# Weights as half units of 512 KB in eight half buffers, norm gains by products, and loads and slots moved

## The chip, the core and the metric

The kernel runs on one core of one Trainium2 chip. The metric is the time of one execution on the device, in microseconds. It is float32 throughout.

## What is computed

A first block and a second block of a transformer run over one sequence of S = 256 tokens with D = 2048 features. The first block has one layer, the second two. Cut to what matters here:

```python
# first block, one layer
h = rms_norm(x, mix_norm_g)                      # gain per feature
proj = h @ w_in                                  # latents, q, k, v of 16 "fox" heads, gates
y_a = causal_block_attention(q_a, k_a, v_a)      # 16 heads from latents, with rope
y_b = causal_block_attention(q_b, k_b, v_b, cum_log_f)
x = x + (concat(y_a, y_b) * sigmoid(gates + b_gate)) @ w_out
h2 = rms_norm(x, ffn_norm_g)
x = x + peer_ffn(h2, ...)                        # see below

# second block, two layers
proj = x @ w_in
ya = diff_attention(...); yb = dilated_attention(...)
yc = conformer_conv(u, glu_gate, ...)            # 31 taps, layer norm over 512 channels, swish
y = concat(ya * silu(ag), yb * silu(bg), yc * silu(cg)) @ w_out
x = layer_norm(ALPHA * x + y, ln_g, ln_b)
```

`peer_ffn` picks, for each token, 8 heads times 16 experts out of 16,384: queries by `w_peer_q`, scores against two sets of 128 keys, the 16 best pairs. Each chosen expert is a row of 2048 numbers of `peer_u` (a dot product with h2, then gelu and the gate's weight) and a row of `peer_v` (added to x with that weight). So each token reads 128 rows of either table.

## The kernel before

**Tiles and passes.** The tokens are two tiles t = 0, 1 of 128. The program is eight passes in this order: `layer1(0)`, `experts(0)`, `layer1(1)`, `experts(1)`, `layer2(0, 0)`, `layer2(1, 0)` (both layers of the second block for tile 0), `layer2(0, 1)`, `layer2(1, 1)`. Each pass streams all its weights from memory. All five engines have an instruction stream written out by hand; semaphores tie them.

**The weight stream.** A unit is a tile of 128 partitions by 2048 floats (8 KB a partition, 1 MB), in the order of `order1` and `order2` (L85 to L111). `STREAM` lists all 612 units with what frees each. SP loads unit u into `ring[:, u % 4]` once PE has used unit u - 4 (L991). On PE `units` (L1339), `out_units` (L1373) and `fin_units` (L1381) wait for a unit and run four matmuls of 512 columns on it: `units` sums a chunk of 512 columns into `psP` over four units, the other two add the merged heads times `w_out` into the four banks of `psO`. ACT or DVE take the chunks. L1339 is hence the line of most matmuls.

**The rows of the experts.** 1024 indirect loads would be one per token and expert; here one gather brings one row for each of the 128 tokens of a tile, 1 MB, so there are 512 gathers: 128 of `peer_u` and 128 of `peer_v` for each tile. POOL issues them in order (L944), each into one of six buffers `rows` or a seventh in `hrow`, once DVE has used the row that was there. DVE uses a row in `slot`: L363 for the dot product, L371 for the addition to `x_sb`. The slots of tile 0 stand among the steps of `layer1(1)` and the start of `experts(1)`, those of tile 1 from there to the end of `layer2(1, 0)`. `stage(m)` opens a stretch of m slots and `mix(f)` runs slots up to the fraction f of it, so a call of `mix` is a point in DVE's order. The counts are tables: `MIX1`, `EMIX`, `MIX2`. In `layer2(l, 0)` each slot is followed by one tap of the convolution (L387) until 31 are done; for tile 1 POOL computes the convolution (L957 to L963).

**The experts' start (tile 1).** `experts(t)` on DVE (from L680) takes transposes, waits for `rsx_ready` (the root of the mean square, by ACT), and forms `hrow` = h2. For t = 0 this is x times the root times a row of gains that was loaded. For t = 1 PE transposes `hT`, which holds x times the gain, back in `rows_back` (L1658) within the second chunk, and DVE multiplies what stands in `psX` by the root (L698). Then come `mix(1.0)` (10 slots) and four rounds of finding the best 16, each of which gives POOL 32 more gathers.

**The convolution's norm.** The mean over 512 channels is a product of `ones` with each of four 128-channel blocks of `cacc` summed in `psX` (L1713), then the same for the squares `csq` (L1718).

**Start and norm rows.** SP loads x of tile 0; ACT loads the identity (L1049) and the 16 columns of `mix_g` (L1050); POOL loads the rest of the constants once x is in. In `layer2(0, 1)` ACT issues, ahead of its first chunk, the bias and counts for the far keys (L1225, L1226) and the four rows `ln_g`, `ln_b` of both layers (L1228).

## Time and profile before

| | us |
|---|---|
| median of 3 runs | 3230.13 |
| lowest, highest | 3229.79, 3232.44 |
| the profiled execution: time | 3231.43 |
| its span, first to last instruction | 3229.6 |
| PE busy | 2475.9 (77%) |
| DVE busy | 1874.4 (58%) |
| POOL busy | 928.7 (29%) |
| ACT busy | 459.2 (14%) |
| bytes moved | 1193.46 MB, 370 GB/s over the span |

The profile is of one execution. Its page gives busy time of the engines and what moved in 40 equal slices of the span; views of the trace give the same for any stretch, list who waited for whom, and print instructions in order of time.
### The profile page before, as it was taken

What the parts mean: (1) busy time and instruction counts of PE and PEld (TensorE: products, weight loads), DVE (VectorE), ACT (ScalarE), POOL (GpSimd) and SP (SyncE); (2) the same over time, 40 slices, a digit from 0 to 9 for tenths busy, and PEclk for the clock granted to TensorE, in tenths of its full rate; (3) what the DMA queues carried; (4) which work ended last, traced back from release to release, by engine and by line L of the source; (5) the groups of instructions that cost most, each with busy time, mean ns of one, the idle gap of its engine ahead of it and who ended that gap; (6) DMA issues with size and microseconds to landing.
All of it is one profiled execution on the core that took longest, in us unless ns stands there. A gap on an engine that the chain in (4) does not pass through costs nothing.

```text
span 3229.6 us, 19340 instructions
## 1 busy us (share of the span) xinstructions
PE 2475.9 (77%) x6564; PEld 1172.0 (36%) x6564; DVE 1874.4 (58%) x2830; ACT 459.2 (14%) x1126; POOL 928.7 (29%) x649
## 2 busy tenths in 40 slices
PE   8999999837757767576788276555645689999998
PEld 4444444413323333233333123222322234444443
DVE  1332333967576576665698857674985653452533
ACT  3222122111101110111101001010100111111111
POOL 0000000345343344333333334431432323500710
PEclk9999999967878888887999698788878889999999
DMA  9888887999999999999999999999999998887886
GB/s 333 279 293 274 286 284 275 418 421 418 421 416 420 422 417 421 422 421 417 356 416 421 404 422 421 422 413 421 421 400 422 421 376 331 290 293 274 279 285 232
DMA packets 169553, 1193.46 MB, mean 370 GB/s; under 512 B 18600, under 2 KB 22328, under 8 KB 25328
## 3 DMA queue, kind: packets, MB, share of 16 engines
q1 hardware_dynamic: 90320, 644.13, 52.6%
q0 software_dynamic: 74192, 538.86, 40.3%
q10 hardware_dynamic: 4944, 9.25, 0.8%
q8 instruction: 52, 0.85, 0.1%
q14 instruction: 45, 0.37, 0.0%
HBM read 1190.07 MB, written 2.10 MB: 369 GB/s over the span
## 4 chain that ended last, share of the span: by engine, by line
DMA 20%; PE 17%; DVE 10%; issue 2%; POOL 2%; ACT 0%; DVEq 0%; ACTq 0%
PE psP L1339 13%; DMA rows<-in_peer_v,tk 11%; DMA rows<-in_peer_u,tk 8%; DVE x_sb L371 3%; PE psO L1373 3%; DVE rows L363 2%; POOL rows L944 2%; DVE work L387 1%; PE psO L1381 1%; DMA hrow<-in_peer_u,tk 1%; DVE hrow L363 0%; DMA ring<-in_w 0%; PE psX L1470 0%; POOL hrow L944 0%; DVE kv L676 0%
## 5 line engine op out<-in xcount | busy, mean ns | idle before, releaser
L1339 PE MATMUL psP<-ring,hT 128*128 128x512 f32 x3584 | 1636.2, 611 | 109.4 <-DMA ring<-in_w 104.8
L1339 PEld LDWEIGHTS psP<-ring,hT 128*128 128x128 f32 x3584 | 685.9, 196 | 990.2 <-issue 812.5
L371 DVE SCALAR_TENSOR_TENSOR x_sb<-rows,tk,x_sb 128x2048 f32<-128x2048 f32 x223 | 524.4, 2351 | 237.8 <-DMA rows<-in_peer_v,tk 218.2
L944 POOL DMA_INDIRECT rows<-in_peer_u,tk x222 | 349.4, 1574 | 1074.6 <-DVEq L732 553.4
L363 DVE CUSTOM_DVE_ANT_0 rows<-rows,hrow 128x2048 f32<-128x2048 f32 x222 | 504.0, 2291 | 207.0 <-DMA rows<-in_peer_u,tk 202.4
L944 POOL DMA_INDIRECT rows<-in_peer_v,tk x223 | 332.5, 1491 | 576.6 <-DVE x_sb L371 511.1
L1373 PE MATMUL psO<-ring,work 128*128 128x512 f32 x832 | 384.2, 615 | 0.5 <-DMA ring<-in_w 0.5
L409 DVE STREAM_TRANSPOSE work<-work 32x128 f32<-32x128 f32 (+1 forms) x640 | 206.4, 323 | 147.4 <-ACT work L1235 87.7
L1373 PEld LDWEIGHTS psO<-ring,work 128*128 128x128 f32 x832 | 161.4, 199 | 187.4 <-issue 186.0
L1480 PE MATMUL psX<-kst,work 128*128 128x128 f32 x68 | 17.9, 415 | 253.0 <-DVEq L526 201.7
L1065 ACT ACTIVATE work<-work,small 128x256 f32<-128x256 f32 (+1 forms) x128 | 56.6, 444 | 481.0 <-DVEq L505 481.0
L1339 PE MATMUL psP<-ring,work 128*128 128x512 f32 (+1 forms) x288 | 114.5, 547 | 8.1 <-DMA ring<-in_w 8.1
L1480 PEld LDWEIGHTS psX<-kst,work 128*128 128x128 f32 x68 | 11.7, 207 | 266.4 <-DVEq L526 211.6
L371 DVE SCALAR_TENSOR_TENSOR x_sb<-hrow,tk,x_sb 128x2048 f32<-128x2048 f32 x33 | 77.6, 2351 | 35.7 <-DMA hrow<-in_peer_v,tk 32.3
L1447 PE MATMUL psX<-kv,work 128*128 128x128 f32 x128 | 28.9, 351 | 85.3 <-DVE kv L512 85.3
L363 DVE CUSTOM_DVE_ANT_0 hrow<-hrow 128x2048 f32<-128x2048 f32 x34 | 77.9, 2290 | 24.8 <-DMA hrow<-in_peer_u,tk 24.1
L1381 PE MATMUL psO<-ring,work 128*128 128x512 f32 x192 | 86.5, 608 | 1.9 <-ACT work L1078 1.4
L523 DVE SCALAR_TENSOR_TENSOR work<-psX,small,work 128x128 f32<-128x128 f32 x96 | 27.0, 345 | 98.3 <-PE psX L1470 97.8
L963 POOL TENSOR_TENSOR work<-work 128x512 f32<-128x512 f32 x60 | 76.3, 1272 | 4.7
L1339 PEld LDWEIGHTS psP<-ring,work 128*128 128x128 f32 x288 | 53.7, 190 | 65.0 <-issue 60.0
L944 POOL DMA_INDIRECT hrow<-in_peer_u,tk x34 | 49.9, 1467 | 86.0 <-DVE tk L363 64.5
L944 POOL DMA_INDIRECT hrow<-in_peer_v,tk x33 | 48.3, 1464 | 84.8 <-DVE x_sb L371 73.0
(352 smaller groups left out, 1622.6 us busy)
## 6 DMA issues: line engine op xcount, KB each, us to landing
ring<-in_w SPq DMA_DIRECT2D x572, 1024.0 KB, 9.0
ring<-in_wq SPq DMA_DIRECT2D x32, 1024.0 KB, 5.0
ring<-in_w SPq DMA_DIRECT2D x8, 512.0 KB, 5.4
rows<-in_peer_v,tk POOLq DMA_INDIRECT x223, 21.6
rows<-in_peer_u,tk POOLq DMA_INDIRECT x222, 20.1
x_sb<-in_x SPq DMA_DIRECT2D x2, 1024.0 KB, 5.9
rows<-in_gate_bias SPq DMA_DIRECT2D x1, 2048.0 KB, 12.2
work<-in_sub_keys ACTq DMA_DIRECT2D x2, 1024.0 KB, 7.9
```

Source lines behind the costliest of these rows:

```text
L363: V.tensor_tensor_reduce(out=row_buf(n), in0=row_buf(n), in1=hrow[:, t, :], scale=1.0, scalar=0.0, op0=ALU.mult, op1=ALU.add, accum_out=do ...
L371: V.scalar_tensor_tensor(out=x_sb[:, t, :], in0=row_buf(n), scalar=dots[t][:, k:k + 1], in1=x_sb[:, t, :], op0=ALU.mult, op1=ALU.add).then ...
L387: own.add(V.scalar_tensor_tensor(out=cacc[:, c, :], in0=convh[:, c, k:k + P], scalar=w, in1=cacc[:, c, :], op0=ALU.mult, op1=ALU.add))
L409: own.add(V.transpose(dst[b_:b_ + 32, :, a_:a_ + 32], src[a_:a_ + 32, :, b_:b_ + 32]))
L944: pool.indirect_dma_start(out=row_buf(n), out_offset=None, in_=a["peer_u" if s < SLOTS else "peer_v"], in_offset=bass.IndirectOffsetOnAxis ...
L963: own.link(T(cacc, cacc, csq, ALU.add))
L1065: ins = A(W4[:, j, :], W4[:, j, :], ACT.Exp, bias=negm[:, 4 * u + j:4 * u + j + 1], accum_out=lsum[:, 4 * u + j:4 * u + j + 1])
L1339: last = MM(psP[:, c % 2, 0:wide], src[:, kk, :], w[:, k, :], start=(kk == 0 and not begun), stop=(kk == 4 * nu - 1))
L1373: last = MM(psO[:, d, :], src[:, k, :], w[:, d, :], start=(bool(first) and k == 0), stop=False)
L1381: last = MM(psO[:, d, :], src[:, k, :], w[:, k, :], start=False, stop=(k == 3))
L1447: last = MM(o, qT[:, j, :], kT[:, j, :], start=(kind != "fox"), stop=(kind != "fox" or bank_ends))
L1480: last = TR(psX[:, 0, P * j:P * (j + 1)], mN[:, P * j:P * (j + 1)], ident)
```

## The change

1. **Half units.** `RING` is 8 buffers of 1024 floats a partition. Each unit becomes two loads and two waits on PE: two matmuls per half. `small` becomes twice 640 floats, `r` twice 512. x of tile 0 comes in two halves too.
2. **Start.** The 16 columns `mix_g` stand beside the identity and come with it in one load; POOL's constants wait for the first half unit, not for x.
3. **Experts of tile 1.** In place of the transposes back, PE forms the gain of every feature in all partitions, 16 matmuls of the broadcast gain columns with the identity into `psO`, between the first two units and the third of its first chunk; DVE multiplies x, root and gain in one operation. Four of the ten slots (`mix(0.4)`) go ahead of it.
4. **Convolution's norm for tile 1.** DVE adds the four blocks up first (two reductions), and PE then needs one matmul for the sum and one for the squares.
5. **Loads one by one.** Bias and counts follow chunk `u`; the four norm rows are issued singly, behind chunks q and v of groups 0 and 1.
6. **Slots moved.** `MIX2` has four fewer in group 1 and four more in group 2 of each layer.

```diff
-RING = 4
+RING = 8
+HALF = UNIT // 2
-MIX2 = [[20, 37, 59], [43, 36, 49]]
+MIX2 = [[20, 33, 63], [43, 32, 53]]
...
+        _h = width(_name) // 2
+        _ended["used"] += 1
+        STREAM.append((_p, _row, 0, _h, "used", _ended["used"]))
         _ended[_how] += 1
-        STREAM.append((_p, _row, width(_name), _how, _ended[_how]))
+        STREAM.append((_p, _row, _h, _h, _how, _ended[_how]))
...
-        ring = sb("ring", [P, RING, UNIT])
+        ring = sb("ring", [P, RING, HALF])
...
                 dve.wait_ge(rsx_ready, t + 1)
                 if t == 0:
                     dve.wait_ge(grow_in, 16)
+                else:
+                    mix(0.4)
                 for d in range(4):
                     w = slice(512 * d, 512 * (d + 1))
                     if t == 1:
-                        dve.wait_ge(h2T_done, d + 1)
-                        V.tensor_scalar(hrow[:, 1, w], psX[:, d % 2, :], rsh[:, 1:2], None, ALU.mult).then_inc(h2T_taken, 1)
-                        continue
-                    own.add(V.scalar_tensor_tensor(out=hrow[:, t, w], in0=x_sb[:, t, w], scalar=rsh[:, t:t + 1], in1=grow[:, w],
-                                                   op0=ALU.mult, op1=ALU.mult))
+                        dve.wait_ge(gain_done, d + 1)
+                    own.add(V.scalar_tensor_tensor(out=hrow[:, t, w], in0=x_sb[:, t, w], scalar=rsh[:, t:t + 1],
+                                                   in1=psO[:, d, :] if t else grow[:, w], op0=ALU.mult, op1=ALU.mult))
                 own.own()
                 if t == 1:
-                    dve.wait_ge(h2T_taken, 4)
+                    dve.sem_inc(gain_taken, 1)
                 mix(1.0)
...
                     if g == 2:
                         mix(0.24 * last)
+                        if t == 1:
+                            dve.wait_ge(conv_done, l + 1)
+                            link(V.tensor_reduce(crs, cacc.rearrange("p c s -> p s c"), AX, ALU.add))
+                            dve.sem_inc(csum_ready, 1)
                         dve.wait_ge(cm_done, r)
                         link(V.tensor_scalar(cmean, psX[:, 1, 0:P], 1.0 / 512, None, ALU.mult))
                         link(V.tensor_tensor(cacc, cacc, over(cmean, CC), ALU.subtract))
                         dve.sem_inc(cc_ready, 1)
                         if t == 1:
+                            dve.wait_ge(csq_ready, r)
+                            link(V.tensor_reduce(cmean, csq.rearrange("p c s -> p s c"), AX, ALU.add))
+                            dve.sem_inc(csum_ready, 1)
                             turn_k(kind, i, l, g)
...
-            pool.wait_ge(x_in, 16)
+            pool.wait_ge(arrived[0], 16)
...
-            sp.dma_start(x_sb[:, 0, :], a["x"][:, 0, :]).then_inc(x_in, 16)
-            for u, (p, row, n, how, count) in enumerate(STREAM):
+            sp.dma_start(x_sb[:, 0, 0:D // 2], a["x"][:, 0, 0:D // 2]).then_inc(x_left_in, 16)
+            sp.dma_start(x_sb[:, 0, D // 2:D], a["x"][:, 0, D // 2:D]).then_inc(x_in, 16)
+            for u, (p, row, at_, n, how, count) in enumerate(STREAM):
...
-                if u == 8:
+                if u == 16:
                     sp.dma_start(x_sb[:, 1, :], a["x"][:, 1, :]).then_inc(x1_in, 16)
...
-                act.dma_start(kst[:, 0:P], a["konst"][:, 0:P]).then_inc(first_in, 16)
-                act.dma_start(cols[:, 0:DC], a["cols"][:, 0:DC]).then_inc(first_in, 16)
+                act.dma_start(kst[:, 0:P + DC], a["konst"][:, 0:P + DC]).then_inc(first_in, 16)
...
-                    for dst, name, at_ in ((ln_g, "ln_g", D), (ln_b, "ln_b", D), (ln_g0, "ln_g", 0), (ln_b0, "ln_b", 0)):
-                        act.dma_start(dst, bass.AP(tensor=a[name].tensor, offset=at_, ap=[[0, P], [1, D]])).then_inc(lnrow_in, 16)
...
+                    if r == 3 and g < 2:
+                        ln_row((ln_g, ln_g0)[g], "ln_g", (D, 0)[g])
...
             def units(c, q0, q1, nu, src, wide=512, begun=False):
-                for q in range(q0, q1):
-                    w = v3(unit()[:, 0:4 * wide], wide)
-                    for k in range(4):
-                        kk = 4 * q + k
-                        last = MM(psP[:, c % 2, 0:wide], src[:, kk, :], w[:, k, :], start=(kk == 0 and not begun),
-                                  stop=(kk == 4 * nu - 1))
-                    last.then_inc(proj_ready if q == nu - 1 else unit_used, 1)
+                for kk in range(4 * q0, 4 * q1):
+                    if kk % 2 == 0:
+                        w = v3(unit()[:, 0:2 * wide], wide)
+                    last = MM(psP[:, c % 2, 0:wide], src[:, kk, :], w[:, kk % 2, :], start=(kk == 0 and not begun),
+                              stop=(kk == 4 * nu - 1))
+                    if kk % 2:
+                        last.then_inc(proj_ready if kk == 4 * nu - 1 else unit_used, 1)
...
+            def gain_over():
+
+                for d in range(4):
                     for j in range(4):
-                        last = TR(psX[:, r % 2, P * j:P * (j + 1)], hT[:, 4 * r + j, :], ident)
-                    last.then_inc(h2T_done, 1)
+                        last = MM(psO[:, d, P * j:P * (j + 1)], col("ffn_g", 4 * d + j).to_broadcast([P, P]), ident, start=True, stop=True)
+                    last.then_inc(gain_done, 1)
...
+                        if t:
+                            pe.wait_ge(csum_ready, 2 * l + 1)
+                            MM(psX[:, 1, 0:P], ones, crs, start=True, stop=True).then_inc(cm_done, 1)
```

The order on PE at the start of `experts(1)`, before; L1351 are the transposes of x, L1339 the query chunks, L1658 the transposes back, L1619 and L1628 the query transposes and the scores of a group:

```order
L1351 MATMUL psX<-kst,x_sb 128x128 x12
L1339 MATMUL psP<-ring,hT 128x512 x4
L1351 MATMUL psX<-kst,x_sb 128x128 x4
L1339 MATMUL psP<-ring,hT 128x512 x16
L1658 MATMUL psX<-kst,hT 128x128 x8
L1339 MATMUL psP<-ring,hT 128x512 x4
L1658 MATMUL psX<-kst,hT 128x128 x8
L1619 MATMUL psX<-kst,work 128x128 x4
L1339 MATMUL psP<-ring,hT 128x512 x4
L1628 MATMUL psO<-work 128x128 x4
```

and after the change:

```order
L1371 MATMUL psX<-kst,x_sb 128x128 x12
L1358 MATMUL psP<-ring,hT 128x512 x4
L1371 MATMUL psX<-kst,x_sb 128x128 x4
L1358 MATMUL psP<-ring,hT 128x512 x4
L1678 MATMUL psO<-kst,cols 128x128 x16
L1358 MATMUL psP<-ring,hT 128x512 x12
L1648 MATMUL psX<-kst,work 128x128 x4
L1358 MATMUL psP<-ring,hT 128x512 x4
L1659 MATMUL psO<-work 128x128 x4
```

The 16 products for the gain stand behind the second unit, and the transposes back are gone.

The order on ACT at the start of `layer2(0, 1)`, before; L1229 and L1230 take chunks `u` and `glu`, L1235 q, L1244 k, L1258 v:

```order
L1295 ACTIVATE small<-small 128x1
L1225 DMA kv<-in_bias_t 128x12x128
L1226 DMA rows<-in_log_count 128x2x128
L1228 DMA rows<-in_ln_g 128x2048
L1228 DMA rows<-in_ln_b 128x2048
L1228 DMA rows<-in_ln_g 128x2048
L1228 DMA rows<-in_ln_b 128x2048
L1229 ACTIVATE work<-psP 128x512
```

and after the change, where those lines are L1238, L1242, L1247, L1258 and L1272:

```order
L1315 ACTIVATE small<-small 128x1
L1238 ACTIVATE work<-psP 128x512
L1240 DMA kv<-in_bias_t 128x12x128
L1241 DMA rows<-in_log_count 128x2x128
L1242 ACT_TABLE_LOAD
L1242 ACTIVATE work<-psP 128x512
L1247 ACTIVATE work<-psP 128x512
L1303 DMA rows<-in_ln_g 128x2048
L1258 ACTIVATE work<-psP 128x512
L1271 ACTIVATE work<-psX 128x4x128
L1272 ACTIVATE work<-psP 128x512
L1303 DMA rows<-in_ln_b 128x2048
```

The first pair of norm rows stands behind q and v of group 0; the second pair stands the same way in group 1.

## Rows read from the trace of the kernel before

**Rows 1.** The page's second part, the span in 40 slices.

```profile
PE   8999999837757767576788276555645689999998
...
GB/s 333 279 293 274 286 284 275 418 421 418 421 416 420 422 417 421 422 421 417 356 416 421 404 422 421 422 413 421 421 400 422 421 376 331 290 293 274 279 285 232
```

**Rows 2.** Windows: stretch, length, busy us by engine, clock, DMA share, GB/s.

```profile
640.00:1520.00 880.00, 586.35 (x1517) 283.08 (x1517) 594.65 (x504) 115.20 (x316) 364.50 (x232) 0.80 1.01 420
1580.00:2640.00 1060.00, 643.79 (x1612) 293.29 (x1610) 784.06 (x1012) 92.40 (x198) 375.69 (x258) 0.84 1.01 418
2940.00:3200.00 260.00, 260.00 (x706) 123.09 (x705) 102.76 (x256) 35.07 (x74) 72.17 (x63) 1.00 0.82 283
```

**Rows 3.** The chain that ended last: start, us, what.

```profile
2730.85 27.66 PE psP L1339 x64
```

**Rows 4.** DMA queues from 563 to 2641 us: packets, MB, share.

```profile
q0 software_dynamic: 73728, 536.90, 62.4%
q1 hardware_dynamic: 44908, 324.55, 37.8%
```

**Rows 5.** PE's waits from 563 to 2641 us: total, times, longest.

```profile
PE psX L1480 <- DVEq L526: 201.7, 12, 28.5
PE psP L1339 <- DMA ring<-in_w: 107.2, 94, 2.7
```

**Rows 6.** The start: DMA issues to landing, and the timeline.

```profile
kst<-in_konst ACTq DMA_DIRECT2D x1, 64.0 KB, 5.4
cols<-in_cols ACTq DMA_DIRECT2D x1, 8.0 KB, 7.5
...
8.84 1.94 PE L1351 MATMUL psX<-kst,x_sb 128*128 128x128 f32 x8 [8.84 <-DMA cols<-in_cols]
```

**Rows 7.** PE's ring wait in the first stage, in the timeline.

```profile
46.93 13.97 PE L1339 MATMUL psP<-ring,hT 128*128 128x512 f32 x32 [1.92 <-DMA ring<-in_w]
```

**Rows 8.** Timeline of the experts of tile 1.

```profile
1542.10 0.20 ACT L1016 ACTIVATE small<-small 128x1 f32<-128x1 f32 x1
...
1557.98 0.66 PE L1619 MATMUL psX<-kst,work 128*128 128x128 f32 x4 [1.07 <-DVE hrow L698]
1558.02 19.54 DVE L371 SCALAR_TENSOR_TENSOR x_sb<-rows,tk,x_sb 128x2048 f32<-128x2048 f32 x8
...
1560.64 3.00 POOL L944 DMA_INDIRECT rows<-in_peer_v,tk  x1 [46.61 <-DVE x_sb L371]
```

**Rows 9.** Windows: 1550 to 1570 us.

```profile
1550.00:1570.00 20.00, 18.93 (x69) 9.94 (x67) 14.38 (x9) 1.28 (x2) 8.45 (x4) 1.00 0.76 271
```

**Rows 10.** Timeline of the convolution's norm, layer 0, tile 1.

```profile
2839.24 1.05 PE L1713 MATMUL psX<-work,kst 128*128 128x128 f32 x8
...
2840.14 7.03 PE L1339 MATMUL psP<-ring,hT 128*128 128x512 f32 x16
```

**Rows 11.** PE at the start of the last stage, the first of three waits.

```profile
2674.95 3.67 PE L1339 MATMUL psP<-ring,hT 128*128 128x512 f32 x8 [1.34 <-DMA ring<-in_w]
```

**Rows 12.** Layer 1 of tile 0: the keys of group 1, and the next window.

```profile
2397.74 2.05 PE L1447 MATMUL psX<-kv,work 128*128 128x128 f32 x8 [42.64 <-DVE kv L512]
...
2400.00:2420.00 20.00, 20.00 (x70) 10.91 (x70) 18.98 (x17) 1.65 (x8) 12.12 (x7) 0.99 0.89 336
```

**Rows 13.** Packets from 38.3 to 44.2 us, and from 44.5 to 50 us.

```profile
DMA packets 931, 2.40 MB, mean 408 GB/s; under 512 B 16, under 2 KB 16, under 8 KB 846
...
DMA packets 324, 2.33 MB, mean 425 GB/s; under 512 B 39, under 2 KB 39, under 8 KB 39
```

**Rows 14.** Packets from 1522 to 1536 us, with ACT's queue.

```profile
DMA packets 2364, 5.50 MB, mean 393 GB/s; under 512 B 110, under 2 KB 1798, under 8 KB 1798
...
q10 hardware_dynamic: 1746, 1.00, 24.3%
```

**Rows 15.** The queues from 1890 to 1920 us.

```profile
q1 hardware_dynamic: 870, 6.35, 51.0%
q0 software_dynamic: 863, 6.29, 50.3%
```

More of the change, by code:

```diff
@@ L48 @@
     NCOLS += _n
-KONST = [("ident", P), ("ones", P), ("tri", P), ("aid", P), ("mask", S), ("iota", TOPK), ("eps6", 1), ("eps5", 1),
+KONST = [("ident", P), ("mix_g", DC), ("ones", P), ("tri", P), ("aid", P), ("mask", S), ("iota", TOPK), ("eps6", 1), ("eps5", 1),
          ("lsc128", 1), ("lsc192", 1), ("one", 1)]
@@ L201, in col @@
         def col(name, i=0):
+            if name == "mix_g":
+                return kst[:, KOL[name] + i:KOL[name] + i + 1]
             return cols[:, COL[name] + i:COL[name] + i + 1]
@@ L1258, in layer2 @@
                     A(value_parts(kind, i, l, t)[-1], taken(("b", l, t, "v", g)), ACT.Copy).then_inc(chunk_taken, 1)
+                    if r == 3 and g < 2:
+                        ln_row((ln_b, ln_b0)[g], "ln_b", (D, 0)[g])
                     if t == 0:
@@ L1363, in x_first @@
                         turn(q + 2)
+                    elif q == 2 and between is not None:
+                        between()
                     units(c, q, q + 1, 4, hT)
@@ L1370, in out_units @@
                 for k in range(k0, k1):
-                    w = v3(unit(), 512)
                     for d in range(4):
-                        last = MM(psO[:, d, :], src[:, k, :], w[:, d, :], start=(bool(first) and k == 0), stop=False)
-                    last.then_inc(unit_used, 1)
+                        if d % 2 == 0:
+                            w = v3(unit(), 512)
+                        last = MM(psO[:, d, :], src[:, k, :], w[:, d % 2, :], start=(bool(first) and k == 0), stop=False)
+                        if d % 2:
+                            last.then_inc(unit_used, 1)
             def fin_units(src):
@@ L1378, in fin_units @@
                 for d in range(4):
-                    w = v3(unit(), 512)
                     for k in range(4):
-                        last = MM(psO[:, d, :], src[:, k, :], w[:, k, :], start=False, stop=(k == 3))
-                    last.then_inc(bank_done, 1)
+                        if k % 2 == 0:
+                            w = v3(unit(), 512)
+                        last = MM(psO[:, d, :], src[:, k, :], w[:, k % 2, :], start=False, stop=(k == 3))
+                        if k % 2:
+                            last.then_inc(bank_done if k == 3 else unit_used, 1)
             def no_a_step():
@@ L1518, in x_here @@
                     if r == 0:
[L1519 to L1520 removed]
+                        pe.wait_ge(first_in, 16)
+                    pe.wait_ge(x_left_in if r < 2 else x_in, 16)
                 if t == 0:
@@ L1527, in layer1 @@
                 c = begin(("a", t, "small", 0))
-                w = v3(unit()[:, 0:1280], 80)
                 for k in range(DC):
-                    last = MM(psP[:, c % 2, 0:80], hT[:, k, :], w[:, k, :], start=(k == 0), stop=(k == DC - 1))
+                    if k % 8 == 0:
+                        w = v3(unit()[:, 0:640], 80)
+                    last = MM(psP[:, c % 2, 0:80], hT[:, k, :], w[:, k % 8, :], start=(k == 0), stop=(k == DC - 1))
+                    if k == 7:
+                        last.then_inc(unit_used, 1)
                 last.then_inc(proj_ready, 1)
@@ L1710, in layer2 @@
                     if g == 2:
[L1711 to L1719 removed]
+                        if t:
+                            pe.wait_ge(csum_ready, 2 * l + 1)
+                            MM(psX[:, 1, 0:P], ones, crs, start=True, stop=True).then_inc(cm_done, 1)
+                        else:
+                            pe.wait_ge(conv_dve, l + 1)
+                            for m in range(CC):
+                                last = MM(psX[:, 1, 0:P], ones, cacc[:, m, :], start=(m == 0), stop=(m == CC - 1))
+                            last.then_inc(cm_done, 1)
+                        units(c, 0, 2, 4, hT)
+                        if t:
+                            pe.wait_ge(csum_ready, 2 * l + 2)
+                            MM(psX[:, 1, P:2 * P], ones, cmean, start=True, stop=True).then_inc(cv_done, 1)
+                        else:
+                            pe.wait_ge(csq_ready, r)
+                            for m in range(CC):
+                                last = MM(psX[:, 1, P:2 * P], ones, csq[:, m, :], start=(m == 0), stop=(m == CC - 1))
+                            last.then_inc(cv_done, 1)
                         units(c, 2, 4, 4, hT)
```

70 lines of the change are left out of this document (26 added, 44 removed).

## The prediction

> **What bounds the kernel now.** Read the page's second part first: its rows cut the span into 40 slices of some 81 us. Three stages show [rows 1]. In slices 1 to 7 and 34 to 40 PE is busy at nine tenths or more in nearly all, its clock nearly whole, and memory delivers 274 to 293 GB/s in most. In slices 8 to 33 PE is at two to eight tenths and memory at 413 to 422 in all but a few. The windows over these stages give the level: 283 GB/s with PE busy all the time, against 420 and 418 GB/s with PE busy 586 of 880 and 644 of 1060 us [rows 2]. So the ends are bound by PE (one unit of 1 MB shows as 8 matmul entries, 27.66 us for 64 of them in the chain, 3.46 us a unit [rows 3], 303 GB/s), and the middle by the DMA engines, which carry 536.9 MB of gathered rows beside 324.55 MB of weights [rows 4]. PE stands idle for some 710 us of the two middle windows, mostly for DVE, whose slots wait for rows (the largest group alone is 201.7 us); for the ring it waits 107.2 us in 94 short waits [rows 5]. What takes DMA time away in the middle, or fills a hole in it, therefore shifts the end one for one; at the ends only what holds PE counts. The profiled execution took 3231.4 us, its span 3229.6; the median of the runs is 3230.1, so 1.3 us come off the sum at the end.
>
> **The change, part by part.** *Start.* PE's first transpose waits for the small load of `mix_g`: it takes 7.5 us to land, the identity's, issued just ahead, 5.4, and PE begins at 8.84 [rows 6]. With `mix_g` in the identity's load, and x in halves, the last to land is that load, some 0.5 us of issue and 2.1 of landing sooner: **2.6 us less**, since PE is busy from there to the experts. Bounds: 0 (the wider load lands as late as the old pair) to 3. POOL's constant loads now wait for the first half unit and not for x, perhaps 1 us later; the first to need them is ACT's root for the first chunk, which PE finishes four units, 14 us [rows 3], after its first, so that is covered.
>
> *Ring at 45 us.* PE waits once for the ring in the first stage, 1.9 us, behind the 3 MB of x and gate bias on SP's queue [rows 7]. The first half of a unit is there 1.25 us before the whole (0.52 MB at 420 GB/s): **1.2 less**, 0 to 1.9.
>
> *Experts of tile 1.* DVE's root is ready when ACT ends at 1542.30, yet the rows are taken up at 1558.02, because DVE stands at the transposes back, and POOL had nothing to gather for 46.61 us [rows 8]. Now four slots stand ahead of that wait. The first can end at 1542.3 + 2.4 = 1544.7, where it ended at 1560.6: gathers restart 16 us sooner. A restart has a ramp, so I count only from 1550 to 1570: 271 GB/s against 421 for 20 us is 3.0 MB, or 7.1 us [rows 9]: **7 less**. Ends: 3 less (more ramp) and 16 less (DVE's own lead, which the DMA rate after 1580 forbids). PE swaps 16 transposes and 1.07 us of waiting [rows 8] for 16 true matmuls at 0.225 us (a group of 4 is followed 0.90 us later [rows 10]), 3.6 us, so at most 2.5 more, in a stretch where DVE and the DMA engines are behind: nothing. The scores of group 0 now wait for DVE to have read the gain from `psO`, which it does near 1555 (four slots of 2.44 us from 1542.3 and four short operations), ahead of PE's transposes for them, which stood at 1557.98 [rows 8].
>
> *Convolution norm of tile 1.* Four sums of 4 matmuls become 4 single ones: 12 times 0.225 us [rows 10], on PE in the last stage, **2.7 less**. DVE adds two reductions. The first waits for nothing but DVE's own order, since POOL's convolution is long done; should it be late, PE stands still. The second must be there when PE has run two units, 6.9 us after the first sums [rows 10]; between them lie a scaling, a subtraction, ACT's square and the reduction, each under 1 us. The key transpositions behind it on DVE start some 1.5 us later, and PE needs them two units and more after that. Hidden; were the cover gone, it would cost twice 1.5 us.
>
> *Norm rows of the second block.* Bias, counts and four rows of 1 MB go out together on ACT's queue, and PE then waits three times for the ring, 1.34, 1.55 and 0.93 us (the first of them: [rows 11]). Now bias and counts follow `u`, and the rows go out singly, a unit or more apart; the ring's cushion of 4 MB is over 13 us of PE. **3.8 less**, bounds 2 and 4.
>
> *Slots moved.* In the second block four slots go from group 1 to group 2 of each layer. PE waited 42.64 us there for the keys, which stood behind DVE's slots with their taps [rows 12]; it now waits behind three fewer (0.6 of 32 slots, not of 36). Only holes in the DMA stream count, and the following 20 us show one: 336 GB/s, 4.0 us [rows 12]. I take half, **2.0 less**, 0 to 4.
>
> *Halves.* Every unit is now two transfers of 4 KB a partition. No row shows such a stream, so it is bounded by its neighbours. While the gate bias loads, 931 packets (16 markers, 830 of 2 KB, so 85 of 8 KB) take 5.9 us; just behind it 324 (285 of 8 KB, 39 markers) take 5.5 us [rows 13]. Over 16 engines a packet of 8 KB costs 88 / 285 = 309 ns; the 830 cost (94.4 - 26.2) / 830 = 82 ns, where a quarter of 309 is 77. A line through both has a fixed part of 6.6 ns. Halving the packets adds one for each 8 KB: 324.55 MB [rows 4] are 39,600 of them, 2,480 per engine, at 6.6 ns **16.3 us more**. The farther neighbour is the bias load with rows of 512 bytes: 393 GB/s over 14 us [rows 14]. Its 5.50 MB less 1.00 leave 4.5 MB, 10.7 us at 421; the 1746 packets took 3.3 us, 30 ns each where the line through zero gives 19: a fixed part of 11 ns, 27 us. Lower end: 0, if the fixed part is hidden at 4 KB. A gain has no source in a stream that is already full. I take the 2 KB neighbour as the nearer one. At the ends memory has a fifth to spare, and nothing is lost. SP issues 1,224 loads in place of 612, at most one each 1.7 us of PE's work, and has nothing else to do. The Trainium skill ("DMA: Bandwidth & Descriptors", Bandwidth) speaks against the change: at least 1 MiB per DMA for three quarters of peak. This trace agrees only in part: four queued loads of 1 MiB reach 425 GB/s here [rows 13], far above the 341 stated there for one, so the size of a single transfer is not what limits. The same page of the Trainium skill (SWDGE vs HWDGE vs iDMA) gives 408.7 GB/s for a stream with rows of 4 KiB; an estimate by that page would be 324.55 MB at 408.7 in place of 425, some 30 us more and not 16.
>
> **Sum:** -2.6 - 1.2 - 7.0 - 2.7 - 3.8 - 2.0 + 16.3 = -3.0. From 3231.4 that is 3228.4, and 1.3 lower by the runs: **3227 us**. 0.2% is 6.5 us, about what a measurement of this kernel tells from no change: 3223.7 to 3236.6.
>
> **The rivals.** *A: packets of 4 KB cost nothing.* Then -19.3 stays: 3211. For it: the fixed part rests on 5.9 us of trace, and 1% of its rate is most of it. Against: both neighbours show one.
>
> *B: the packet costs as by the bias load,* 27 us: 3238.
>
> *C, slower: the share of the queues tips.* Where both queues are full, the two take turns packet by packet: 870 and 863 packets, 6.35 and 6.29 MB in 30 us [rows 15]. If weights bring 4 KB a turn and gathers 8, weights fall from 211 GB/s to 140, and a unit comes every 7.5 us, not 5.0. Each of the 94 ring waits grows by 2.5 us, 235 us in all. PE's other idle time, 600 us, covers most, and the DMA engines stay full while row buffers are free. It decides once DVE stands before PE with all seven full: then memory runs at PE's 303 of 421 GB/s and 28% is lost. With a quarter of the 235 us in that state it costs 16 us: 3243. The Trainium skill, "DMA: Bandwidth & Descriptors" (Queues, rings and completion order), has engines alternate between rows packet by packet; the trace agrees (870 against 863). It also has packets span several descriptors, by which the share need not follow the row's length.
>
> *D: the experts' hole stays,* since rows for the last slots land no sooner: 7 us back, 3234.
>
> **How the numbers follow.** Forecast 0.37 (own range 3219 to 3236), A 0.26, B 0.13, C 0.14, D 0.10. Faster: A whole and 0.11 of the forecast, 0.37. Slower: most of B and C and a little of D and the forecast, 0.27. Same: 0.36. The range leaves out a tenth at each side: 3208 to 3246.
>
> **What the profile after would show.** PE's first transpose near 6.2 us. POOL's longest gap in the experts of tile 1 near 30 us, not 46.6. No ring waits in the 50 us behind the last gather. In the middle the rate, now 418 to 420 GB/s over the long windows: 415 to 417 for the forecast, unchanged for A, 413 for B. For C: in stretches with both queues full twice as many bytes gathered as loaded, ring waits well over 107 us, and windows far under the stage's rate. Wrong outright, whatever the time, if the rate is the same and the gathers' restart is not.

## The result and the profile after

The change made the kernel slower: 3237.9 us median (3234.8 to 3242.3) against 3230.6 before (3227.3 to 3238.1), 17 runs each, a ratio of 1.0022 with a 95% interval of 1.0014 to 1.0029. Forecast were 3227 us and a range of 3208 to 3246: the time lies in the range, but the kernel is slower where a gain of 3 us was forecast. The profiled execution took 3242.3 us, the slowest of the 17; its span is 3240.2, where that of before was 3229.6. So the two traces differ by 10.6 us and the medians by 7.3.

The page of the kernel after, its second part, then the chain by line:

```profile
PE   9999999847666667566877555555665679999998
...
PEclk9999999978999999998999999999999999999999
...
GB/s 340 277 296 275 283 285 276 410 418 418 417 417 416 417 417 414 417 416 415 365 410 386 416 417 417 417 417 417 416 417 417 416 367 325 315 299 273 280 292 229
...
DMA ring<-in_w 38%; PE psP L1358 29%; PE psO L1396 7%; DMA rows<-in_peer_u,tk 7%; PE psO L1406 2%; DVE rows L369 2%; DMA ring<-in_wq 2%; DVE x_sb L377 1%; POOL rows L957 1%; PE psX L1473 1%; PE psX L1496 1%; PE psX L1371 1%; PE psX L1470 1%; PE psX L1469 0%; DMA rows<-in_peer_v,tk 0%
```

The three stages stand as before [rows 1], but no slice of the middle reaches 422 any more: the best are 418 and most 417. The chain (the work that ended last, followed back step by step) now runs over the ring for 38% of the span. PE's waits in the middle of the kernel after (line, what for: total, times, longest):

```profile
PE psP L1358 <- DMA ring<-in_w: 500.9, 305, 2.8
PE psO L1396 <- DMA ring<-in_w: 71.7, 46, 1.9
PE psX L1506 <- DVEq L532: 26.3, 2, 16.4
```

They answer to [rows 5]. PE waited 201.7 us for DVE at one place and 107.2 us for the ring; it now waits some 570 us for the ring and 26.3 for DVE in the largest such group. The queues from 1890 to 1920 us, after, against [rows 15]:

```profile
q0 software_dynamic: 1144, 8.32, 66.8%
q1 hardware_dynamic: 1141, 4.15, 34.7%
```

Still packet by packet, 1144 against 1141, and so two bytes gathered for each one loaded: the share that rival C named is there. The start, in PE's timeline:

```profile
5.04 1.97 PE L1371 MATMUL psX<-kst,x_sb 128*128 128x128 f32 x8 [5.04 <-DMA kst<-in_konst]
...
41.03 3.71 PE L1557 MATMUL psP<-ring,hT 128*128 128x80 f32 x16 [2.11 <-DMA ring<-in_w]
```

PE begins 3.8 us sooner than in [rows 6], yet waits 2.11 us at 41 us where it waited 1.92 at 47 [rows 7], and the first gather is issued at 562.1 us, 1.0 sooner.

**A ledger.** The stage between the first gather and PE's first transpose of tile 1's second block is bound by DMA and carries 864.0 MB (536.9 of rows, 324.4 of weights, 2.7 of the rest; after), and within 1 MB as much in the other kernels with the same gathers. Its length splits into the bytes at the full rate of that kernel's packets (422 GB/s with packets of 8 KB, 417 with weights in 4 KB, both shown below) and holes, the remainder: the time that would be over if memory had run at that rate throughout. The row of a kernel adds up to its span:

| kernel | first stage | bytes at full rate | holes | last stage | span |
|---|---|---|---|---|---|
| before | 563.1 | 2047.4 | 31.3 | 587.8 | 3229.6 |
| after | 562.1 | 2071.9 | 27.3 | 578.9 | 3240.2 |
| whole | 561.8 | 2047.4 | 26.2 | 580.8 | 3216.2 |
| halves | 565.2 | 2071.9 | 23.7 | 586.6 | 3247.4 |
| pieces | 564.9 | 2071.9 | 27.7 | 579.2 | 3243.7 |
| slots | 562.8 | 2047.4 | 22.9 | 579.5 | 3212.6 |
| oldexp | 560.4 | 2047.4 | 29.1 | 580.6 | 3217.5 |
| halves_exp | 561.0 | 2071.9 | 22.0 | 578.1 | 3233.0 |
| whole_exp | 561.0 | 2047.4 | 25.0 | 579.6 | 3213.0 |
| whole_late | 557.4 | 2047.4 | 27.3 | 580.7 | 3212.8 |
| best | 557.8 | 2047.4 | 23.5 | 579.0 | 3207.7 |

So after against before is -1.0 at the start, +24.5 by the rate, -4.0 in holes and -8.9 in the last stage. Each row is one execution, and kernels with the same start differ by up to 2.4 us in the first column, so differences under 3 us in a cell prove nothing. Between a kernel with packets of 8 KB and one with 4 KB the cut between rate and holes is no sharper: the streams alone moved 421.9 and 417.5 GB/s before rounding, and with these two the term for the rate is 22 us and not 24.5, and the holes of `after` are as many as before.

### The profile page after: what moved, and what is told of

It is laid out like the page before. It is cut to its first block, busy times and chain, and to the rows that moved or that the text cites. A ratio compares the mean times of both kernels' runs of the same rounds, so it can differ in the third digit from the quotient of the medians.

```text
span 3240.2 us, 19946 instructions
## 1 busy us (share of the span) xinstructions
PE 2488.9 (77%) x6556; PEld 1124.8 (35%) x6556; DVE 1881.8 (58%) x2834; ACT 458.5 (14%) x1126; POOL 908.9 (28%) x649
## 4 chain that ended last, share of the span: by engine, by line
DMA 47%; PE 44%; DVE 7%; issue 1%; POOL 1%; ACT 1%; DVEq 0%; ACTq 0%
DMA ring<-in_w 38%; PE psP L1358 29%; PE psO L1396 7%; DMA rows<-in_peer_u,tk 7%; PE psO L1406 2%; DVE rows L369 2%; DMA ring<-in_wq 2%; DVE x_sb L377 1%; POOL rows L957 1%; PE psX L1473 1%; PE psX L1496 1%; PE psX L1371 1%; PE psX L1470 1%; PE psX L1469 0%; DMA rows<-in_peer_v,tk 0%
## 5 line engine op out<-in xcount | busy, mean ns | idle before, releaser
L1358 PE MATMUL psP<-ring,hT 128*128 128x512 f32 x3584 | 1664.5, 610 | 481.0 <-DMA ring<-in_w 461.6
L1358 PEld LDWEIGHTS psP<-ring,hT 128*128 128x128 f32 x3584 | 659.7, 193 | 1414.8 <-issue 743.8
L957 POOL DMA_INDIRECT rows<-in_peer_u,tk x222 | 294.6, 1327 | 1128.0 <-DVEq L738 550.5
L957 POOL DMA_INDIRECT rows<-in_peer_v,tk x223 | 362.3, 1625 | 527.0 <-DVE x_sb L377 464.6
L1396 PEld LDWEIGHTS psO<-ring,work 128*128 128x128 f32 x832 | 153.0, 193 | 268.3 <-issue 173.2
L1358 PE MATMUL psP<-ring,work 128*128 128x512 f32 (+1 forms) x288 | 124.7, 575 | 39.3 <-DMA ring<-in_w 39.3
L957 POOL DMA_INDIRECT hrow<-in_peer_v,tk x33 | 58.0, 1757 | 82.2 <-DVE x_sb L377 76.4
L393 DVE SCALAR_TENSOR_TENSOR work<-work,cols 128x128 f32<-128x128 f32 x240 | 68.0, 346 | 0.0
L972 POOL TENSOR_TENSOR work<-work,cols 128x512 f32<-128x512 f32 x62 | 65.2, 1052 | 4.9
```

The source lines that it names most:

```text
L393: own.add(V.scalar_tensor_tensor(out=cacc[:, c, :], in0=convh[:, c, k:k + P], scalar=w, in1=cacc[:, c, :], op0=ALU.mult, op1=ALU.add))
L957: pool.indirect_dma_start(out=row_buf(n), out_offset=None, in_=a["peer_u" if s < SLOTS else "peer_v"], in_offset=bass.IndirectOffsetOnAxis ...
L972: own.link(T(cacc if k == 0 else csq, moved, wk_, ALU.mult))
L1358: last = MM(psP[:, c % 2, 0:wide], src[:, kk, :], w[:, kk % 2, :], start=(kk == 0 and not begun), stop=(kk == 4 * nu - 1))
L1396: last = MM(psO[:, d, :], src[:, k, :], w[:, d % 2, :], start=(bool(first) and k == 0), stop=False)
```

## The experiments

Each but the first was timed beside the kernel before on its own chip; ratios are against that, with 95% intervals. The kernels of the first four runs shared 11 runs of before (3231.1), of the next four 13 (3230.0), of the last four 15 (3230.7).

**1. The streams alone.** No engine computes; SP loads 48 units in each of four forms, then loads run beside gathers.

```diff
+load(i, flat[:, UNIT * i:UNIT * (i + 1)], a["w1"][u])
...
+load(i, flat[:, 1024 * i:1024 * (i + 1)], a["w1"][u // 2][:, 1024 * (u % 2):1024 * (u % 2 + 1)])
```

> This kernel computes nothing of the reference: it only loads. Four stretches of 48 MB of weights alone (units of 1 MB with 8 KB a partition; halves of 512 KB with 4 KB; units of 1 MB whose rows land as two pieces of 4 KB; units whose rows land as four pieces of 2 KB), four units in flight, then units of 8 KB and then halves beside 48 gathers of 1 MB. Packet theory (a packet has a fixed cost): rates fall with the packet, about 422, 414, 415 and 405 GB/s, the same for halves and for two pieces. Transfer theory (the cost is that of a transfer and its completion): halves are slower than whole units and the pieces are not. Share theory (the queues take turns by packet): beside gathers, whole units get half of the bytes and halves a third.

Windows of the run with the streams alone: whole units, halves, whole units in two pieces, in four; then whole units beside gathers, and halves beside gathers (stretch, length, busy us, clock, DMA share, GB/s):

```profile
20.00:110.00 90.00, 0.00 (x0) 0.00 (x0) 1.00 1.01 422
135.00:225.00 90.00, 0.00 (x0) 0.00 (x0) 1.00 1.03 410
270.00:370.00 100.00, 0.00 (x0) 0.00 (x0) 1.00 1.03 410
380.00:500.00 120.00, 0.00 (x0) 0.00 (x0) 1.00 1.05 387
530.00:720.00 190.00, 0.00 (x0) 35.60 (x38) 1.00 1.01 422
790.00:900.00 110.00, 0.00 (x0) 27.19 (x29) 1.00 1.02 417
```

The queues of the last two, 530 to 720 us and 790 to 900 us:

```profile
q1 hardware_dynamic: 5512, 40.18, 50.8%
q0 software_dynamic: 5506, 40.00, 50.5%
...
q0 software_dynamic: 4204, 30.60, 66.9%
q1 hardware_dynamic: 4204, 15.31, 34.8%
```

Transfers of 512 KB and transfers of 1 MB in two pieces both run at 410: over this range the packet's size counts, not how many transfers there are. Over 16 engines a packet takes 310.6 ns at 8 KB, 159.8 at 4 KB and 84.7 at 2 KB. So the fixed part is 2 x 159.8 - 310.6 = 9.0 ns, and 9.6 between 4 and 2 KB. The forecast of 422, 414, 415 and 405 GB/s had the order right and the cost of a small packet too low. The second pair of queues shows 4204 packets against 4204, as the share theory had it.

**2. Halves alone, halves left out, and their packets alone.** In `whole` all other edits stay and the ring holds four whole units. `halves` is the kernel before with nothing but the halves. `pieces` is `whole` with each load in two 4 KB pieces a partition:

```diff
-ring = sb("ring", [P, RING, UNIT])
+ring = sb("ring", [P, 2, RING, UNIT // 2])
...
-sp.dma_start(ring[:, u % RING, 0:n], src[:, at_:at_ + n]).then_inc(arrived[u % RING], 16)
+sp.dma_start(ring[:, :, u % RING, 0:n // 2], v3(src[:, 0:n], n // 2)).then_inc(arrived[u % RING], 16)
```

> The changed kernel with whole units of 1 MB in four buffers; all other edits stay. If halves are what costs (rate of the middle back from 417 to 421 GB/s, queues half and half, PE no longer late at the last gather): about 3212 us, 0.6% under the kernel before, ring waits in the middle near 110 us and not 600. If one of the other edits is to blame (the new hole at 1680 to 1760 us, the moved slots), halves cost only their 16 us: 3222 or more, and the hole stays.

> The kernel before with halves in eight half buffers and nothing else. If halves cost by the rate (22 us over the middle) and by PE's lateness at the last gather (12 us): 3255 to 3265 us. If only by the packet, 3247. If their finer grain pays for part, under 3245. PE late by 10 to 20 us within the passes of the middle in each case of the share theory.

> As the run named whole, but each row of a unit lands as two pieces of 4 KB, so packets are as in the changed kernel while there are half as many transfers, semaphores and waits. If packets make both the rate and the share: as the changed kernel, 3238 us within 4, ring waits of some 600 us. If the number of transfers costs, between whole and the changed kernel. If the finer grain of halves helps, slower than the changed kernel.

Measured: whole 3216.6 us (0.9957, 0.9945 to 0.9970), halves 3246.8 (1.0050, 1.0037 to 1.0063), pieces 3243.8 (1.0039, 1.0027 to 1.0051). That is 5 us over the 3212 forecast for `whole`, on the 3247 of the packet alone for `halves`, and 2 us above the band around 3238 for `pieces`. The other edits are a gain of 14.6 us. The halves cost 16 us on the kernel before and 21 on top of the other edits (1.0022 against 0.9957, +-5); the two don't differ for certain. The packets alone, with whole transfers and whole buffers, cost 27 us. The finer buffers may give some 6 of them back (3237.9 against 3243.8, with intervals that overlap).

In `whole` PE's waits are those of before (line, what for: total, times, longest):

```profile
PE psX L1498 <- DVEq L528: 197.3, 12, 28.2
PE psP L1355 <- DMA ring<-in_w: 121.1, 100, 2.6
```

The ring waits of `after`, 500.9 us against 121.1 here, thus belong to the halves. They belong to their packets: `pieces` has whole transfers and waits once a unit, and its ring waits in this group are 382.8 us, in 159 waits, and its queues from 1890 to 1920 us share by packets too, 1118 gathered against 1119 loaded. But most of them only take the place of PE's idleness for DVE. What they leave can be seen at two places. The windows of `after` from 1680 to 1760 us and from its last gather to the last stage, then the latter of `whole`:

```profile
1680.00:1760.00 80.00, 66.80 (x160) 29.41 (x160) 56.30 (x109) 9.75 (x25) 19.83 (x13) 0.94 0.97 379
...
2618.00:2661.00 43.00, 34.76 (x75) 13.78 (x74) 17.15 (x8) 1.19 (x2) 0.94 (x1) 0.93 0.95 365
```

```profile
2606.70:2635.40 28.70, 23.74 (x52) 10.46 (x52) 16.78 (x8) 0.60 (x1) 1.13 (x1) 0.91 1.01 422
```

When the gathers end, PE has more units before it in `after`: 43.0 us in place of 28.7, and toward the end PE is the slower one, so memory gives 365 GB/s. That is 43 x (1 - 365/417) = 5.4 us of holes; the dip from 1680 on is 80 x (1 - 379/417) = 7.3. Yet `whole` has as many holes in all (26.2 against 27.3), at other places.

The ledger also says how 16 and 21 us can both come of the same halves. Between the traces of before and `halves` it has +24.5 for the rate and -7.6 in holes; between `whole` and `after` it has +24.5 and +1.1. One of the places is that of [rows 12], layer 1 of tile 0, where PE waits for the keys. The windows from 2380 to 2420 us of before, `halves`, `slots` (experiment 4: `whole` with the old table of slots) and `whole`, with the waits of PE for these keys in the last three:

```profile
2380.00:2420.00 40.00, 22.26 (x79) 13.21 (x80) 38.81 (x44) 1.65 (x8) 17.46 (x12) 0.74 0.95 378
...
2380.00:2420.00 40.00, 22.87 (x78) 13.82 (x78) 39.12 (x55) 2.84 (x10) 12.27 (x11) 0.79 1.01 415
...
2380.00:2420.00 40.00, 29.52 (x95) 17.53 (x96) 38.56 (x37) 3.53 (x10) 21.65 (x13) 0.79 0.96 386
...
2380.00:2420.00 40.00, 34.63 (x108) 18.46 (x108) 37.91 (x41) 4.13 (x11) 20.38 (x13) 0.92 1.01 414
```

```profile
2407.36 2.05 PE L1455 MATMUL psX<-kv,work 128*128 128x128 f32 x8 [12.85 <-DVE kv L516]
...
2390.48 2.05 PE L1465 MATMUL psX<-kv,work 128*128 128x128 f32 x8 [42.97 <-DVE kv L514]
...
2382.83 2.04 PE L1465 MATMUL psX<-kv,work 128*128 128x128 f32 x8 [34.35 <-DVE kv L514]
```

The halves fill that hole by themselves (415 of 417 GB/s), and with whole units the new table of slots fills most of it (414 of 422, against 386): what both fill can be gained once. No run takes the halves with the new table and nothing else, so this is read from traces and not tested by a time.

**3. The share of the turn.** Gathered rows in two halves as well, with halves for weights (`both4`) and with whole units (`rows4`):

```diff
+half_rows = a["peer_u" if s < SLOTS else "peer_v"].rearrange("r (h w) -> (r h) w", h=2)
+for h in range(2):
+    pool.indirect_dma_start(out=row_buf(n)[:, 1024 * h:1024 * (h + 1)], out_offset=None, in_=half_rows,
+                            in_offset=bass.IndirectOffsetOnAxis(ap=(eid, odd)[h][t][:, k:k + 1], axis=0)).then_inc(row_in[b], 16)
```

> The changed kernel, but each gathered row of 8 KB also comes as two rows of 4 KB (1,024 indirect DMAs of 512 KB in place of 512 of 1 MB), so that both queues have packets of one size again. Theory R (the halves cost their packets' fixed time alone): the gathers' 537 MB now pay it too, so the middle falls from 417 to about 410 GB/s, and the time rises from 3237.9 to 3250 to 3265 us, although TensorE's waits for the ring fall back to about 120 us. Theory S (the halves cost their place in the turn between the queues, and with it TensorE's punctuality): the waits fall to about 120 us and the time falls below the changed kernel's, to 3225 to 3235 us, in spite of the lower rate.

> Whole units (8 KB packets, four buffers, all other edits), but the gathered rows come as 4 KB packets: the share of the turn tips the other way, to the weights. Theory R: the fixed time is paid on 537 MB in place of the halves' 324 MB in the middle, so the loss against 3216.6 us is 537/324 of the halves' 21 us, near 35 us: 3250 us. Theory S: the weights are always early, TensorE waits no more than 120 us for the ring, and the time stays within 15 us of the whole units' 3216.6: under 3232 us.

Measured: both4 3299.7 us (1.0218, 1.0204 to 1.0231), rows4 3352.2 (1.0391, 1.0375 to 1.0406). Neither theory had this. The page of `both4`, its first part and its rates:

```profile
PE 2479.7 (75%) x6556; PEld 1159.5 (35%) x6556; DVE 1881.2 (57%) x2842; ACT 459.2 (14%) x1126; POOL 1670.6 (51%) x1161
...
GB/s 343 287 287 273 283 279 299 409 376 391 409 390 409 409 409 407 409 397 392 398 409 409 384 398 403 410 409 410 388 395 410 409 395 319 312 299 269 281 293 226
```

POOL's busy time went from 908.9 to 1670.6 us: an indirect DMA costs POOL as much for half a row as for a whole one, and the chain is POOL's for 31% of the span, where it was 1% in `after`. So the experiment doesn't separate the theories by time. Two things it does show. The best slices stand at 410 here and at 415 in `rows4`, which is the packet law once more (all 864 MB in 4 KB, and 537 of them). And with equal packets PE's ring waits on its largest group fall from 461.6 to 80.3 us (344.0 in `pieces`, where gathered rows have the larger packets, and 3.0 in `rows4`, where weights have). That is as the share has it, though POOL, which now holds the gathers back, may be part of it. Why `rows4` is 52 us slower than `both4` was not followed up.

**4. The other edits one by one.** `slots` is `whole` with the old table; `oldexp` is `whole` with the transposes back and DVE's four products, and no slots ahead of them.

```diff
-MIX2 = [[20, 33, 63], [43, 32, 53]]
+MIX2 = [[20, 37, 59], [43, 36, 49]]
```

> Whole units and all other edits, with the table of slots in layer 2 as it was before. By the prediction's term of -2.0 for the moved slots this is 2 us slower than with the new table: 3218.6 us. Rival: the trace with whole units loses 10 of its 14 us of lead between gathers 256 and 320, the first passes of layer 2; if the new table does that, this kernel is 3 to 8 us faster: 3209 to 3214 us.

> Whole units and all other edits, but the weights of the expert rows of tile 1 made as before (transposes back out of hT, four products by DVE, no slots ahead of them). By the prediction's term of -7.0 it is 3223.6 us. Rival: the lead at gather 250 says that the edit alone brings 12 us, so 3228.6 us. Second rival: what it gains is given back in layer 2, where the gathers are bound by DMA, and the time is within 2 us of 3216.6.

Measured: slots 3215.5 us (0.9956, 0.9943 to 0.9970), the same as `whole` within some 6 us: a cost of 2 us, as forecast, isn't seen in the time, nor is it excluded. The traces show it in its place. From 1600 to 2600 us, which holds most of layer 2 for tile 0, `slots` moves 417.80 MB and `whole` 418.92, which is 2.7 us at 422 GB/s, and PE's wait for the keys is 42.97 against 34.35 us. `best` against `whole_late` has the same sign (418.01 MB against 419.42). What hides it is the stretch ahead, from 1500 to 1600 us, which the table doesn't touch: 392 GB/s in `slots`, 378 in `whole`. Why it differs is open. oldexp 3221.2 (0.9973, 0.9963 to 0.9983): the experts' edit is worth 4.7 us, give or take 5, which excludes the rival's 12 but not 7, nor the second rival's 2. In `whole` POOL's gap there is 34.17 us, and the gather behind it is issued at 1545.9 us, as the forecast said (1544.7). In `after` it is later, in POOL's timeline:

```profile
1554.24 3.00 POOL L957 DMA_INDIRECT rows<-in_peer_v,tk  x1 [37.21 <-DVE x_sb L377]
```

PE reaches the experts' transposes 6 us later there (1534.3 against 1528.2), ACT's root follows, and DVE's first slot starts at 1551.6 and not at 1543.3. Half of the edit's lead is gone (the gather came at 1560.6 before).

**5. A wait that neither had before.** In `after` DVE stands for the exponential of tile 1's gates, in its timeline:

```profile
1710.58 0.29 DVE L747 TENSOR_REDUCE small<-tk 128x8 f32<-128x128 f32 x1 [20.21 <-ACT tk L1269]
```

It was 0.4 us before, 3.1 in `halves`, 6.5 in `whole` and 20.9 in `pieces`, so the packets are enough for it. DVE comes earlier by the experts' edit (at 1690.4 us in `after`, 1705.3 in `halves`); ACT, in program order behind the copy of a chunk of PE's, later by the halves (it starts the exponential at 1710.2 us in `after`, 1689.6 in `whole`). Two kernels take the exponential ahead of that copy, and two more take the 3 MB behind unit 8 apart.

```diff
+if g == 0 and r == 1:
+    act.wait_ge(top_sub, 2)
+    A(gates[1], gates[1], ACT.Exp).then_inc(top_exp, 1)
 A(k_raw, taken(("b", l, t, "k", g)), ACT.Copy).then_inc(chunk_taken, 1)
...
 if g == 0:
-    if r == 1:
-        act.wait_ge(top_sub, 2)
-        A(gates[1], gates[1], ACT.Exp).then_inc(top_exp, 1)
...
-if u == 8:
+if u == 48:
     sp.dma_start(x_sb[:, 1, :], a["x"][:, 1, :]).then_inc(x1_in, 16)
+if u == 14:
     sp.dma_start(v3(bgrow, 512), bass.AP(tensor=a["gate_bias"].tensor, offset=1024, ap=[[0, P], [1536, 8], [1, 512]])).then_inc(bgrow_in, 16)
```

> The changed kernel with one instruction moved: ScalarE's exponential of tile 1's gates stands ahead of the k chunk's copy in the first pass of layer 2, not behind it. In the changed kernel VectorE waits 20.2 us for it, and the bytes moved between 1,680 and 1,760 us fall to 379 GB/s. Theory L (TensorE's lateness under the halves turns into that wait through ScalarE's order): the wait falls to about 6 us, the dip goes, and the time falls by 4 to 8 us, to 3230 to 3234. Rival: the total is bytes over rate from the first gather to the last stage, and the dip is made up elsewhere, so under 2 us of change: 3236 to 3240.

> The same move with whole units, where VectorE's wait is 6.5 us and no dip is seen. Theory L: no more than 2 us faster than 3216.6, so 3214.5 to 3217. If it gains as much as with halves, the wait has a price of its own and the interplay of the edits is not explained by it.

> Whole units and all other edits, but the loads of x's tile 1 (1 MB) and the gate bias (2 MB) stand behind units 48 and 14 of SP's queue, not both behind unit 8. By the prediction TensorE's earlier start and the end of the ring wait at 45 us are worth 3.8 us in the first stage, of which 1.3 came; if the burst of 3 MB is what turned the rest into a wait of 2.5 us at 43.9 us, the first gather moves from 561.8 to about 559.3 us and the time from 3216.6 to 3214. Rival: the first stage is held by other waits and nothing moves.

> Whole units, the old table of slots, the exponential moved and the two loads apart: what each gave together. If they add up: 3211 to 3214 us, against 3230 before and 3238 with the change. If the slots and the exponential stand in for each other: 3215.

Measured: halves_exp 3235.2 us (1.0014, 1.0005 to 1.0023), 2.8 less than `after` with intervals that overlap, between theory L (3230 to 3234) and its rival (3236 to 3240): the time decides for neither. The profile tells more. DVE's wait and the dip in `halves_exp`:

```profile
1693.62 0.29 DVE L747 TENSOR_REDUCE small<-tk 128x8 f32<-128x128 f32 x1 [5.45 <-ACT tk L1260]
```

```profile
1680.00:1760.00 80.00, 66.51 (x168) 28.43 (x167) 54.73 (x100) 9.76 (x25) 18.19 (x13) 0.99 1.01 402
```

The wait fell from 20.2 to 5.5 us, the window rose from 379 to 402 GB/s, and the holes fell by 5.3 us. With whole units the move did nothing (3216.8; 0.9959, 0.9945 to 0.9973), as theory L had it.

whole_late gave 3210.6 us (0.9939, 0.9925 to 0.9952), 6 us under `whole` where 2.6 were expected; the intervals just meet, and the trace gives 4.4 us to the first stage. PE's timeline there has no ring wait in the first stage, at the place of the two above:

```profile
35.54 2.31 PE L1356 MATMUL psP<-ring,hT 128*128 128x512 f32 x5
37.69 3.69 PE L1549 MATMUL psP<-ring,hT 128*128 128x80 f32 x32
41.22 9.22 PE L1356 MATMUL psP<-ring,hT 128*128 128x512 f32 x21
```

The first gather comes at 557.4 us, 5.7 before that of the kernel before: about the 3.8 of the start and the 1.9 of the old wait. `best` gave 3210.2 (0.9935, 0.9922 to 0.9949), the same as whole_late within the intervals, and at the lower end of what was expected of the parts together. It is the fastest kernel of the study, 20.4 us under the kernel before in its own comparison and some 28 under the change.

## Why the prediction was wrong

*Halves, +16.3: mis-sized, and the largest error.* The step that failed is the fixed part of 6.6 ns a packet, taken from 931 packets beside the loading of the gate bias [rows 13]. The stream alone shows 9.0, and 2,480 packets per engine make 22 us of that; by the rounded rates, 864.0 MB at 417 and not at 422, it is 24.5, and by the unrounded ones 22 again. The mechanism and the count were right. That `halves`, against the kernel before, cost 16 us to the number is luck: its trace has the larger price, less 7.6 us of holes that the prediction had not ("a gain has no source in a stream that is already full"). On top of the other edits, as here, it was 21. The weakness was named (rival A: 1% of the rate is most of it) but not used: a window of 5.9 us can't carry a term of 16 us. The farther neighbour, 11 ns [rows 14], was about as near. By the Trainium skill ("DMA: Bandwidth & Descriptors", SWDGE vs HWDGE vs iDMA) a stream of 4 KiB rows runs at 408.7 GB/s; the stream alone gave 410. The page's figure was right. The estimate of 30 us was too high because I set it against 425; against 422 it would have been 25.

*Start and ring at 45 us, -3.8: came to -1.0* (0.3 to 2.7 by the spread of kernels with this start). PE did begin 3.8 us sooner, more than forecast. The step that failed is to count the start and the ring apart. A PE that starts sooner meets the same burst of 3 MB sooner, and the half unit's 1.25 us didn't help. `whole_late` shows 5.7 once the burst is away. Seen the other way, PE's pace until 45 us was set by those loads and not by PE.

*Experts of tile 1, -7.0: -4.7 with whole units* (the 7 lies within its uncertainty). The time of the restart was right in `whole` and 8 us late in `after`, since ACT's root waits for PE, which the halves had made late. The prediction took PE as unchanged there. Its price was taken from a hole that would be gone, but the gap was only cut from 46.61 to 34.17 us. From 1500 to 1600 us memory moved 365 GB/s before, 369 in `oldexp` and 378 in `whole`: 2 to 3 us of full rate.

*Slots moved, -2.0: right at its place with whole units, nothing in the time.* With whole units the hole of [rows 12] shrinks as forecast, and the stretch gains 2.7 us, though by the ledger the holes of `slots` (2633.1 - 562.8 - 2047.4 = 22.9) are in all no more than those of `whole`. The step that failed is to add this term to that of the halves: with halves and the old table the hole is gone already (415 GB/s in `halves`), so in `after` there was none to fill.

*Convolution norm and norm rows, -6.5: right.* The last stage is 7.0 us shorter in `whole` and 8.9 in `after`. PE no longer stops where it had stopped three times for the ring [rows 11]. (The sign "no ring waits in the 50 us behind the last gather" failed all the same: from the last gather at 2618 to 2643 us `after` has six such waits, 8.2 us in all, before any norm row is loaded.) Its timeline in `after`:

```profile
2666.99 53.38 PE L1358 MATMUL psP<-ring,hT 128*128 128x512 f32 x124
```

*Rival C: the share.* Its mechanism is there, 2 bytes to 1, with ring waits of 570 us, where its sum had 107 and 235. Its price was not: the extra waits took the place of PE's waits for DVE, and 27.3 us of holes are no more than before. It added 5.4 us ahead of the last stage and part of the dip at 1700 us, which fewer holes elsewhere offset. *Rival B* (27 us, 3238) has the time, by luck in part: its price is 3 to 5 us too high, and it keeps 19.3 us of gains where 14.6 came. *Rivals A and D* are refuted: the rate fell, and the restart came.

By the times alone the account closes: the other edits gained 14.6 us and not 19.3, and the halves cost 21 on top of them and not 16, which makes +7 in place of -3; the two errors are about as large. By the parts: with 22 in place of 16, 1 in place of 4, 5 in place of 7 and 0 in place of 2 the sum would have been 22.3 - 1.0 - 4.7 - 6.5 = +10.1 and not -3. The medians moved by 7.3 us and the spans of the profiled executions by 10.6. What stays open: whether the halves cost more on top of the other edits than alone (21 against 16, each with about 4 to 5 us of uncertainty), though the 20 us wait and the hole that two edits fill give reasons for it; and what the finer buffers are worth apart from packets.

## What to carry to other kernels

In a stage bound by DMA, first write the stage as bytes over the rate of its packets, plus holes. A change of the packet's size alters the first term for the whole stage, and here 1.2% of 2 ms outweighed what finer buffers brought. Two edits that fill the same hole gain it once. Where two queues alternate by packet, cutting one queue's packets also cuts its share, and engines in program order behind the slower stream become late at places where they had slack.

## What the runs showed of the hardware

The clock of PE rose with the halves: in the window from 1760 to 2560 us the granted clock was 0.97 in `after` and 0.82 in `whole`. PE stood still in long waits for DVE in `whole` (up to 28.2 us) and mostly in waits under 3 us for the ring in `after`. In `pieces` most of the waits for DVE are gone as well, but the ring waits are half as many and up to 4.5 us long, and its clock is 0.84. So fewer waits for DVE alone don't raise it; no run tests more. The windows of `after`, `whole` and `pieces`:

```profile
1760.00:2560.00 800.00, 473.69 (x1144) 190.54 (x1144) 576.64 (x620) 71.50 (x156) 275.71 (x209) 0.97 1.02 417
```

```profile
1760.00:2560.00 800.00, 458.70 (x1152) 211.25 (x1152) 561.54 (x591) 69.28 (x147) 287.12 (x206) 0.82 1.01 418
```

```profile
1760.00:2560.00 800.00, 525.99 (x1143) 229.29 (x1144) 576.78 (x625) 71.47 (x156) 254.37 (x208) 0.84 1.01 415
```

0.97 is nearly all of the stretch at 2.4 GHz, 0.82 has more of it at 1.2 GHz. The better clock bought no time, since memory set the pace of both.

Not expected either: two DMA streams with 8 KB rows and with 4 KB rows share by packets (4204 to 4204), and the number of transfers is free in the range tried (410 GB/s with 512 KB and with 1 MB of the same packets), while the preparation of an indirect DMA is paid per instruction (POOL's busy time of 1670.6 us for 1,024 halves against 908.9 for 512 whole rows).
